# Head-norm sums and spreads placed between pairs of k tiles of blocks 93 to 99

## The reference

```
xn = rmsnorm(x, norm_mix)
proj = xn @ w_in
u, q, k, v, qi, ki, wi, gl = jnp.split(proj, np.cumsum(IN_SIZES).tolist(), axis=-1)
q = rope(rmsnorm(q.reshape(nb, s, N_HEADS, HEAD_DIM), q_norm), pos)
k = rope(rmsnorm(k.reshape(nb, s, N_KV_HEADS, HEAD_DIM), k_norm), pos)
...
gates = jax.nn.sigmoid(gl.astype(jnp.float32)).reshape(nb, s, N_BRANCH, D_MODEL)
```

## Time and profile before

| | |
|---|---|
| median of 3 runs | 3043.86 us (3041.05 to 3045.55) |
| profiled execution | 3041.63 us |
| its span, first to last instruction | 3039.8 us |
| mean granted TensorE clock | 0.998 |
| TensorE busy | 2994.0 us, 98% |
| VectorE busy | 1965.2 us, 65% |
| ScalarE busy | 1247.8 us, 41% |
| the stretch in layer 1 | from 348.47 us (first rank matmul) to 385.77 us (first scan output) |
| the same in layer 2 | from 1858.24 us to 1898.61 us |

### The profile page before, as it was taken

One profiled execution on the slowest core, in us unless ns is written; L12 is line 12 of the kernel. 1 busy time (PEld: TensorE's weight loads), 2 busy tenths in 40 slices (PEclk: granted clock), 3 DMA queues, 4 the chain that ended last, 5 costly groups with the idle time before them and its releaser, 6 DMA issues. The chain is left out here.

```text
span 3039.8 us, 58606 instructions
## 1 busy us (share of the span) xinstructions
PE 2994.0 (98%) x23480; PEld 2852.2 (94%) x23480; DVE 1965.2 (65%) x3141; ACT 1247.8 (41%) x1767; POOL 253.3 (8%) x239
## 2 busy tenths in 40 slices
PE   8999999999999999999999999999999999999999
PEld 7988888999999999999988888889999999999999
DVE  7559888577655545555575697885776565455653
ACT  4443333544554333334344422344445443333332
POOL 4320000400000000000043200013000000000000
PEclk9999999999999999999999999999999999999999
DMA  7547444745655655556555473447556555555564
GB/s 253 164 145 203 145 141 145 243 167 178 196 185 182 199 172 174 185 181 206 187 194 167 149 204 126 143 163 230 170 177 199 182 183 198 167 181 181 185 205 135
DMA packets 150191, 546.45 MB, mean 180 GB/s; under 512 B 19824, under 2 KB 25072, under 8 KB 149520
## 3 DMA queue, kind: packets, MB, share of 16 engines
q1 hardware_dynamic: 137296, 507.40, 50.0%
q0 software_dynamic: 12096, 35.67, 4.6%
q10 hardware_dynamic: 640, 1.16, 0.1%
HBM read 536.95 MB, written 7.21 MB: 179 GB/s over the span
## 5 line engine op out<-in xcount | busy, mean ns | idle before, releaser
L1790 DVE TENSOR_TENSOR w_ffn_low<-ring_ffn,w_ffn_high 128x1024 fp32r<-128x1024 f32 (+1 forms) x480 | 638.8, 1332 | 456.0 <-ACT w_ffn_high L1300 456.0
L1300 ACT ACTIVATE w_ffn_high<-ring_ffn 128x1024 fp32r<-128x1024 f32 (+1 forms) x480 | 547.9, 1142 | 641.8 <-PE main L1013 640.9
L1011 PE MATMUL main<-x_ffn_high,w_ffn_high 128*128 128x264 f32 x2816 | 792.1, 281 | 0.0
L1013 PE MATMUL main<-x_ffn_high,w_ffn_low 128*128 128x264 f32 x2816 | 791.7, 281 | 0.0
L1012 PE MATMUL main<-x_ffn_low,w_ffn_high 128*128 128x264 f32 x2816 | 791.7, 281 | 0.0
L1011 PEld LDWEIGHTS main<-x_ffn_high,w_ffn_high 128*128 128x128 f32 x2816 | 526.8, 187 | 0.1
L1012 PEld LDWEIGHTS main<-x_ffn_low,w_ffn_high 128*128 128x128 f32 x2816 | 526.8, 187 | 0.1
L1013 PEld LDWEIGHTS main<-x_ffn_high,w_ffn_low 128*128 128x128 f32 x2816 | 526.8, 187 | 0.0
L1013 PE MATMUL main<-hidden_high,w_ffn_low 128*128 128x264 f32 x1408 | 395.8, 281 | 0.0
L1011 PE MATMUL main<-hidden_high,w_ffn_high 128*128 128x264 f32 x1408 | 395.8, 281 | 0.0
L1012 PE MATMUL main<-hidden_low,w_ffn_high 128*128 128x264 f32 x1408 | 395.8, 281 | 0.0
(11 more groups left out here) (373 smaller groups left out, 4767.7 us busy)
## 6 DMA issues: line engine op xcount, KB each, us to landing
ring_ffn<-in_w_up SPq DMA_DIRECT2D x352, 512.0 KB, 3.2
ring<-in_w_in SPq DMA_DIRECT2D x260, 512.0 KB, 3.4
ring_ffn<-in_w_down SPq DMA_DIRECT2D x128, 704.0 KB, 4.1
ring<-in_w_br SPq DMA_DIRECT2D x64, 512.0 KB, 3.9
ring<-in_w_out SPq DMA_DIRECT2D x64, 512.0 KB, 3.1
w_low<-in_w_in POOLq DMA_DIRECT2D x20, 512.0 KB, 6.9
ring<-in_w_glu SPq DMA_DIRECT2D x16, 512.0 KB, 3.7
out_x<-x SPq DMA_DIRECT2D x8, 528.0 KB, 5.9
```

The lines of the kernel that those rows point to most:

```text
L1011: mm(out, wfh[:, slot, w], high[:, kk, :], start=kk == 0, stop=False)
L1013: m = mm(out, wfl[:, slot, w], high[:, kk, :], start=False, stop=kk == chunks * kts - 1)
L1300: af(wfh[:, s, 0:cols], ring_ffn[:, s, 0:cols], ACT.Copy).then_inc(high_ready, 1)
L1790: tt(wfl[:, s, 0:cols], ring_ffn[:, s, 0:cols], wfh[:, s, 0:cols].bitcast(F32), ALU.subtract).then_inc(low_ready, 1)
```

## The change

On TensorE the 12 sums no longer stand in rows of 6, 3 and 3, nor the 12 spreads in two rows of 6. After each of them come two k tiles of a unit (`pair`, six float32r matmuls): sums 0 to 3 carry unit 93, sums 4 to 7 unit 94, sums 8 to 11 unit 95; unit 96 stands whole between the last sum and the first spread; spreads 0 to 3 carry unit 97, 4 to 7 unit 98, 8 to 11 unit 99. The two groups of rank matmuls come without a unit behind them. Units 96 to 105 get other places for their high parts, and with this ScalarE and VectorE make the parts of some units at other points of their order; the wait for `gix_ready` now stands on ScalarE behind the root. What is computed stays the same.

```diff
-LATE = {92: 0, 93: 1, 94: 0, 95: 1, 96: 2, 97: 3, 98: 0, 99: 2, 100: 3, 101: 0, 102: 2, 103: 3, 104: 0, 105: 2}
+LATE = {92: 0, 93: 1, 94: 0, 95: 1, 96: 0, 97: 1, 98: 2, 99: 3, 100: 0, 101: 2, 102: 3, 103: 0, 104: 2, 105: 3}
...
@@ TensorE @@
                             mm(side[1 + g][:, 0:n * (NK + 1)], rank_of[:, h * P:(h + 1) * P],
                                per_seq[:, 3 * g:3 * g + n, :].rearrange("p b n -> p (b n)"), start=True, stop=True).then_inc(spread_ready, 1)
-                        fill(1)
+
+                    def pair(n):
+                        nonlocal filled
+                        w_in_piece(filled // 2, filled % 2 * 8 + n % 4 * 2, 2)
+                        filled += n % 4 == 3
 
                     def sum_heads(first, last):
                         for t in range(first, last + 1):
...
                             mm(side[0][0:NHK, 0:T], one_hot[:, NHK - 1 - t:2 * NHK - 1 - t], sq[:, t % 2, :],
                                start=t == 0, stop=t == NHK - 1).then_inc(qsum_ready, 1)
+                            pair(t)
 
                     spread_rows(0)
                     sum_heads(0, 5)
                     spread_rows(1)
-                    sum_heads(6, 8)
+                    sum_heads(6, NHK - 1)
                     fill(1)
-                    sum_heads(9, NHK - 1)
-                    fill(2)
                     pe.wait_ge(spread_used, 6)
                     for t in range(NHK):
...
                         mm(side[t % 4][:, 0:T], ident[0:NHK, t:t + 1].to_broadcast([NHK, P]), rs[0:NHK, 0, :],
                            start=True, stop=True).then_inc(qinv_spread, 1)
-                        if t in (5, NHK - 1):
-                            fill(1)
+                        pair(t)
@@ ScalarE @@
                         if t == 5:
                             evac_gates(46, 1)
                             highs_to(95)
-                        if t == 10:
-                            act.wait_ge(gix_ready, 1)
+                        if t == 9:
                             highs_to(96)
-                        if t == 11:
-                            highs_to(97)
-                            evac_gates(47, 1)
                     load_root()
                     act.wait_ge(qsum_ready, NHK)
                     af(rs[0:NHK, 0, :], side[0][0:NHK, 0:T], ACT.Sqrt, bias=small[0:NHK, 7:8], scale=1.0 / HD).then_inc(qstd_ready, 1)
-                    highs_to(98)
+                    highs_to(97)
+                    evac_gates(47, 1)
+                    act.wait_ge(gix_ready, 1)
                     highs_to(99)
                     evac_gates(48, 1)
@@ VectorE @@
                         dve.sem_inc(pick_step, 1)
-                        lows_to(93)
+                        lows_to(94)
                         for h in range(2):
-                            if h == 1:
-                                lows_to(94)
                             for g in range(3):
...
                                 if h == 1 and g == 1:
                                     lows_to(95)
                         dve.sem_inc(gix_ready, 1)
-                        lows_to(97)
+                        lows_to(96)
...
                     v.reciprocal(rs[0:NHK, 0, :], rs[0:NHK, 0, :]).then_inc(qinv_ready, 1)
 
-                    lows_to(98)
+                    lows_to(97)
                     for t in range(12):
-                        if t == 6:
-                            lows_to(99)
+                        if t in (2, 6):
+                            lows_to(98 + t // 6)
                         dve.wait_ge(qinv_spread, t + 1)
```

## The result

The changed kernel takes **3050.88 us** (median of 16 runs, 3049.26 to 3052.21), the kernel before 3043.94 (16 runs, 3041.00 to 3045.93): 6.9 us more, ratio 1.0024 with a 95% interval of 1.0018 to 1.0031. The forecast was 3050.3.

The account below looks back on a forecast made before the run. TensorE, busy for 98% of the span, was taken to bound the kernel. From the profiled 3041.63 us, +11.7 for shape changes, waits saved and a new wait, and -3.1 for the clock, gave 3050.3 us; range 3044 to 3056.

Parts of the forecast that it names:

- The price of a change of tile shape: TensorE, going to a small tile and back: 0.28 us per lone sum, 0.38 us per lone spread.
- the rotations: Two TensorE matmuls with 128x128 tiles like the projection's: 0.88 us for two of 0.445, so going there and back is free.
- Rival (a): Lone small matmuls on TensorE pay for one shape change only, not slower: 3040 us; chance 0.18.
- The waits for the squares: TensorE's sums waiting for ScalarE's squares: four waits of 0.24 us a layer go, covered by pairs of k tiles.
- The new wait: TensorE waits for unit 95's low part, about 0.5 us a layer (bounds 0 and 0.9).
- The other covers: Other unit parts, VectorE's products and the scan's output stay hidden; root and reciprocal with 0.7 us to spare.
- The sum: Per layer, sums of squares 1.56, spreads 3.80 and new wait 0.5 make 5.86 us; both layers +11.7 us.
- The clock: Layer 2's two half-clock stretches behind the rows of spreads go: -3.06 us, bounds 0 and -3.06.
- rival (b): TensorE's clock falls with small tiles however placed: 3053.3 us, some 1.5 more per further fall, to 3057; chance 0.12.
- The total: Whole kernel: 3041.63 + 11.7 - 3.1 = 3050.3 us, +6.4 us (0.21%) against the median.

## Why the prediction was right, point by point

- **The price of a change of tile shape** is the core of it, and it held: 0.30 for a lone sum (0.28 forecast) and 0.385 for a lone spread (0.38). That it is the shape, not the float32 type and not loneness, was argued from the rotations and is now shown: with full tiles 12 spreads a layer lose 43.42 - 38.72 = 4.7 us (4.56 forecast). Rival (a), that a lone matmul pays for one change only, is out; both changes stand in the timeline. The page "TensorEngine Tiling (Array Packing)" of the Trainium skill says in Key Properties that each change of mode drains TensorE; the runs with full tiles agree, in that the price is gone where the shape stays the same. The page gives no price, and whether the time is that of a drain no run here shows.
- **The waits for the squares** went as forecast, and the pairs cover them.
- **The new wait** at unit 95 was 0.44 us for 0.5, and the edit that took it away confirmed its cause.
- **The other covers held**: no wait for unit 96 or 97, for a product or at the scan's output. Unit 97's low part was done at 373.6 us, and TensorE wanted it at 374.6, so the spare was 1.0 us for a forecast 0.4. In the kernel with only the spreads between pairs, where the last sum has no pair behind it, that cover did not do and the wait of 0.36 us came.
- **The sum**: 6.1 us in layer 1 for 5.86. Each sum with its pair takes 1.47 us instead of 1.455, which over 12 is the missing 0.2. Two sums of the working were off without touching this one: the terms of rival (a) add up to 1.3 us a layer, not 0.8, which puts it at 3041.1 instead of 3040 us, and 0.24, 0.445 and 0.28 are 0.97, not 0.98.
- **The clock**: 3.1 us came back in layer 2 (it grew by 3.04, layer 1 by 6.12), as forecast, and rival (b) is out for this kernel: no fall in the stretches of two profiles and no group of runs ten microseconds above the others in 27. But the reason was incomplete. I took lone spreads with a pair behind each to be safe. In the profiles the clock fell among them only behind a wait and did not come back until they were over, and a wait at the first of them went with 10 us more in seven of ten runs (3049 against 3060) and, by the run times, with one or two falls in all five runs where it was longer. The page "TensorE: Matmul & The Clock Gate" of the Trainium skill, section What's actually happening, ties the half rate to an idle engine. The falls at 373.3 and at 1897.8 us have a wait ahead of them, of 0.36 and some 1.8 us; the falls behind the rows, and the 30 us at half, came with TensorE busy throughout, and there the runs decide against idleness as the whole story.
- **The total**: 3050.3 forecast, 3050.88 measured. Part of that closeness is luck, since single executions differ by 3 us. From profile to profile the two stretches grew by 9.2 us for a forecast 8.6, and the whole execution by 10.6. The forecast started from a profiled execution 2.3 us below the median of the kernel before and added nothing for this, since falls not seen in the profile would go too. By the medians, with 6.1 us for each of the two stretches, 3043.94 + 12.2 - 3050.88 = 5.3 us came back instead of 3.1. Further falls in the median execution would fit the 2.2 us between them, but no profile near 3044 us shows any.

In one line: the change took away eight waits of 0.24 us and, in the profiled execution, 3.1 us of slow clock, and it made TensorE go to another tile shape and back ten times more per layer for the spreads and nine times more for the sums. 10 x 0.385 and 9 x 0.30 in two layers are 13.1 us; less 1.9 for the waits and with 0.9 for the new ones that is 12.1, against 2 x 6.1 measured.

## What to carry to other kernels

A small matmul set among large ones cost here 0.445 us by its length and another 0.30 or 0.385 by its shape. Giving it its neighbours' tile, with zeros for the rows or columns it lacks, took the second part away; where that is impossible, keep such matmuls together. With equal tiles, interleaving them with other work is a way to hide waits; with unequal ones it cost more than the waits it hid. Where narrow tiles take turns with full ones, look at the clock of more than one run, and keep the weights well ahead of the first of them.

## What the runs showed of the hardware that was not expected

- A float32 matmul of 264 columns between float32r ones costs 0.445 us and nothing for the change of type, where its tile is 128x128 like theirs.
- TensorE's clock fell to 1.2 GHz behind a row of six 12-row spreads (2.9 us, engine busy) in four of six stretches of the kernel before, and in both of the kernel with only the sums between pairs. With 128-row tiles, nearly all zeros, it fell in none of ten stretches at the same place (five profiles of four kernels). Only two of these ten have the spreads in rows; in the other eight they stand alone, where 12-row spreads without a wait kept the clock too (six stretches of three profiles). That the number of rows decides is therefore suggested, not shown; nothing between 12 and 128 rows was tried.
- Once at half, the clock stayed there for 30.6 and 34.0 us while 12-row spreads took turns with six full matmuls each, and came back only behind them. Behind the rows of spreads it came back after 3 to 7 us.
